# Loads moved ahead of phase barriers, and weight units split five and six groups ahead

## The reference, cut to what matters

```python
mod = jax.nn.silu(c) @ w_ada[l] + b_ada[l]
shift, scale, gate = jnp.split(mod[:, None, :].astype(F32), 3, axis=-1)
h = (rms_norm(x, g_pre[l]) * (1.0 + scale) + shift).astype(x.dtype)
if l % 2 == 0:
    y, s1, s2 = mixer_ab(h, ...)   # gated linear attention and retention, 4 + 4 heads
else:
    y, s1, s2 = mixer_c(h, ...)    # causal convolution of width 4, then gated delta rule
x = (x.astype(F32) + gate * rms_norm(y, g_post[l])).astype(x.dtype)
```

## Time and profile before

| | us |
|---|---|
| median of 3 runs | 2666.85 (2664.86 to 2667.93) |
| profiled execution, its own time | 2668.84 |
| its span, first to last instruction | 2667.1 |
| PE busy in the span | 2482.0 (93%) |
| DVE busy | 1320.2 (50%) |
| ACT busy | 926.3 (35%) |
| POOL busy | 796.3 (30%) |
| mean granted clock of TensorE, share of full | 0.965 |

### The profile page before, as it was taken

The page is one execution under the profiler, slowest core; times in us unless marked ns, Lnnn a source line. Parts: engine busy times, 40 slices in busy tenths (PEclk is TensorE's granted clock), DMA queues, the critical chain, the costliest instruction groups (busy, mean ns, idle before and its releaser), DMA issues. The chain is left out here.

```text
span 2667.1 us, 53838 instructions
## 1 busy us (share of the span) xinstructions
PE 2482.0 (93%) x21052; PEld 1495.8 (56%) x21052; DVE 1320.2 (50%) x2927; ACT 926.3 (35%) x2664; POOL 796.3 (30%) x848
## 2 busy tenths in 40 slices
PE   7999999997899986989999999985899999999998
PEld 2444444444566632434444444455788787887876
DVE  3412112111687743981643626424666566665666
ACT  3534242322111113432322322234445454554541
POOL 2531001021111103551010000005555556465564
PEclk8999999998999996989999999997999999999998
DMA  8451212033544543542121111116513222231213
GB/s 294 132 157 48 83 45 75 32 117 124 209 146 157 173 162 114 162 135 77 64 72 52 64 52 52 56 48 174 136 58 107 63 81 89 65 105 57 81 46 92
DMA packets 256585, 270.37 MB, mean 101 GB/s; under 512 B 31223, under 2 KB 189959, under 8 KB 256378
## 3 DMA queue, kind: packets, MB, share of 16 engines
q1 hardware_dynamic: 184858, 217.28, 25.1%
q10 hardware_dynamic: 71520, 50.13, 6.7%
HBM read 180.00 MB, written 87.36 MB: 100 GB/s over the span
## 5 line engine op out<-in xcount | busy, mean ns | idle before, releaser
L613 PE MATMUL inc_b<-raw_next,inc_w_hi 128*128 128x512 bf16 (+1 forms) x768 | 229.7, 381 | 0.5 <-ACT inc_taps L1977 0.5
L613 PE MATMUL inc_b<-keep,inc_w_hi 128*128 128x512 bf16 (+1 forms) x768 | 228.5, 379 | 0.0
L613 PE MATMUL inab_b<-inab_wt,keep 128*128 128x512 f16 x768 | 167.1, 379 | 4.3 <-POOL inab_wt L562 4.1
L613 PE MATMUL inab_b<-inab_wt,inab_h 128*128 128x512 f16 x768 | 166.4, 379 | 0.0
L1131 PE MATMUL mixab_y<-keep,mixab_oT_hi 128*128 128x512 f16 x512 | 152.5, 379 | 7.9 <-DVE mixab_f_y L1211 6.2
L2089 DVE SCALAR_TENSOR_TENSOR inc_acc<-inc_ub,inc_taps,inc_acc 128x512 f32<-128x512 f32 x192 | 152.1, 792 | 6.8
L2085 DVE COPY inc_ub<-inc_halo 128x3 f32<-128x3 f32 x96 | 21.5, 223 | 252.6 <-ACT inc_ub L1996 252.6
L613 PE MATMUL inc_b<-raw_next,inc_w_lo 128*128 128x512 bf16 x384 | 146.1, 381 | 0.0
L613 PE MATMUL inc_b<-keep,inc_w_lo 128*128 128x512 bf16 x384 | 145.6, 379 | 0.0
L1996 ACT ACTIVATE inc_ub<-inc_b 128x512 f32<-128x512 f32 x96 | 57.0, 594 | 252.6 <-PE inc_b L613 252.6
L613 PEld LDWEIGHTS inab_b<-inab_wt,keep 128*128 128x128 bf16 (+1 forms) x768 | 74.8, 98 | 95.6 <-issue 6.0
(11 more groups left out here) (523 smaller groups left out, 6108.5 us busy)
## 6 DMA issues: line engine op xcount, KB each, us to landing
tmp_qkv<-inc_so SPq DMA_DIRECT2D x96, 256.0 KB, 2.0
mixc_qkv<-tmp_qkv SPq DMA_DIRECT2D x15, 1536.0 KB, 7.7
inc_stage<-in_w_in_c ACTq DMA_DIRECT2D x32, 512.0 KB, 4.5
inab_stage<-in_w_in_ab ACTq DMA_DIRECT2D x24, 512.0 KB, 4.1
mixab_cw<-in_w_ada ACTq DMA_DIRECT2D x6, 2048.0 KB, 14.6
inab_wt<-in_w_ada SPq DMA_DIRECT2D x10, 1024.0 KB, 14.5
keep<-in_x_prompt SPq DMA_DIRECT2D x16, 512.0 KB, 4.2
tmp_v<-inab_vz SPq DMA_DIRECT2D x32, 256.0 KB, 3.9
```

Of the source, the lines that this page charges most:

```text
L613: last = nc.tensor.matmul(dst, lhs(a, k), rhs(b, k), start=(k == 0 and i == 0), stop=(k == KT - 1 and i == len(PASSES) - 1))
```

## The change

- `load_tables` joins names that lie side by side in HBM into one transfer (new function `runs`), and the names are reordered for it: 3 transfers become 1 and 7 become 1 in phase_in_ab, 7 names become 4 in 2 transfers in phase_mix_ab, 3 names become 2 in 1 transfer in phase_in_c. The tables ident, sel and sel_s stay resident in `tab0`.
- `raw_next` is allocated in phase_in_ab, in place of inab_h, and takes the first tile of phase_mix_ab ahead of the barrier (a third buffer); tile 2 is loaded at the start of phase_mix_ab.
- `stage_next` is allocated in phase_mix_ab, in place of the first ring tile, and takes units 0 and 1 of w_in_c and the rows of conv_c once four pieces of w_ada are multiplied. In phase_in_c it is also the room of inc_so and inc_zb.
- The waits of PE for tables at the start of both phases go; in phase_in_c one stands later.
- In groups 3 and 10 of the first block two units are split (`TWICE`), so from group 3 on the split is five groups ahead and from group 10 on six.

```diff
 def load_tables(eng, sem, dst, names, table_d):
...
+    for c0, w in runs(names):
+        eng.dma_start(dst[:, at:at + w], table_d[:, c0:c0 + w]).then_inc(sem, 16)
+        at += w
+
+
+def runs(names):
+
+    out = []
     for n in names:
         c0, w = TABLE[n]
-        eng.dma_start(dst[:, at:at + w], table_d[:, c0:c0 + w]).then_inc(sem, 16)
-        at += w
+        if out and sum(out[-1]) == c0:
+            out[-1] = (out[-1][0], out[-1][1] + w)
+        else:
+            out.append((c0, w))
+    return out
...
-    first_names = ["ident", "sel", "sel_s"]
+    first_names = ["sel", "sel_s", "ident"]
...
+    raw_next = io["raw_next"] = io["keep"].enter_context(nc.sbuf_tensor("raw_next", [P, KT, BLK], F32))
...
+    pre = [raw_flat[:, i * D:(i + 1) * D] for i in range(3)] + [raw_flat[:, 3 * D:3 * D + 8]]
+    io["first_tile"] = pre
...
         outputs(nb - 1, BLK, TPB, [])
         rot_load(nb, NS)
+        sp.wait_ge(mm, G * nb)
+        for i in range(4):
+            sp.wait_ge(vz_out[i], 16 + 16 * TPB)
+        sp.dma_start(pre[0].rearrange("p (g n) -> p g n", g=8), io["qk0"][:, :, 0:P].rearrange("g p n -> p g n")).then_inc(pre_in, 16)
+        sp.dma_start(pre[1], io["v0"][0:P, :]).then_inc(pre_in, 16)
+        sp.dma_start(pre[2], io["z0"][0:P, :]).then_inc(pre_in, 16)
+        sp.dma_start(pre[3], io["dec0"][:, 0, :]).then_inc(pre_in, 16)
         outputs(nb, NS, 1, [])
+        sp.wait_ge(pre_in, 64)
...
+def in_c_stages(room):
+
+    flat = room[:].rearrange("p k n -> p (k n)")
+    return [flat[:, i * D:(i + 1) * D].rearrange("p (k n) -> p k n", k=KT) for i in range(2)], flat[:, 2 * D:3 * D]
...
-    names = ["ident", "incl", "incl_s", "seq", "sel", "sel_s", "eye_h"]
+    names = ["incl", "incl_s", "seq", "eye_h"]
...
-        load_tile(sp, 0, 0, P)
+        sp.sem_inc(tile_in[0], 64)
         load_tables(sp, tab_in, tab, names, io["table"])
         load_tile(sp, 1, 1, P)
...
+        load_tile(sp, 2, 0, P)
...
-        turn(0, 0, 0, P, P)
...
         fin.load_sample(sp, io["x_sample"], io["gate_s"][0], 0, gate_in)
+        stages, rows_c = in_c_stages(stage_next)
+        sp.wait_ge(cond.mm, 4)
+        for unit, stage in enumerate(stages):
+            sp.dma_start(stage, io["w_in_c"].rearrange("(k p) n -> p k n", p=P)[:, :, unit * P:(unit + 1) * P]).then_inc(next_in, 16)
+        for i in range(3):
+            sp.dma_start(rows_c[32 * i:32 * i + CONV, :], io["conv_c"][:, i * D:(i + 1) * D]).then_inc(next_in, 16)
...
     def _(pe):
-        pe.wait_ge(tab_in, 16 * len(names))
         ident = tv["ident"]
...
-            tile(t, t, 0)
+            tile(t, (2, 1)[t], 0)
...
+    TWICE = (3, 10)
+    units_at = [range(AHEAD + g + sum(t < g for t in TWICE), AHEAD + g + 1 + sum(t <= g for t in TWICE)) for g in range(G)]
...
         prep.first_tiles_done(sp)
         load_tables(sp, tab_in, tab, names, io["table"])
-        for i in range(3):
-            sp.dma_start(rows[32 * i:32 * i + CONV, :], io["conv_c"][:, i * D:(i + 1) * D]).then_inc(rows_in, 16)
+        sp.sem_inc(rows_in, 48)
+        for i in range(2):
+            sp.sem_inc(weights.stage_in[i], 16)
...
-            weights.lo(pool, AHEAD + g)
+            for u in units_at[g]:
+                weights.lo(pool, u)
...
-        for unit in range(weights.slots - 1):
-            weights.load(act, unit)
-        weights.hi(act, 0)
+        weights.hi(act, 0, False)
...
                 if first:
-                    weights.hi(act, AHEAD + g)
+                    for u in units_at[g]:
+                        weights.hi(act, u)
```

More of the change, by code:

```diff
@@ L945, in _ @@
             cond.add(dve, n)
-        dve.wait_ge(tab_in, 16 * len(names))
+        dve.wait_ge(tab_in, 16 * len(runs(names)))
         for g in range(2):
@@ L1017, in _ @@
     def _(pe):
-        pe.wait_ge(first_in, 16 * len(first_names))
+        pe.wait_ge(first_in, 16 * len(runs(first_names)))
         pe.wait_ge(silu, 1)
@@ L1029, in _ @@
         cond.pair(pe, 2)
-        pe.wait_ge(tab_in, 16 * len(names))
+        pe.wait_ge(tab_in, 16 * len(runs(names)))
         pe.wait_ge(small_in, 32)
@@ L1321, in phase_mix_ab @@
     dec = [ph.sb(f"dec{i}", [P, 8]) for i in range(2)]
+    for room, a, g in zip((qk, v, z), io["first_tile"], (8, H, H)):
+        room.append(a.rearrange("p (g n) -> p g n", g=g))
+    dec.append(io["first_tile"][3])
     ktok = ph.sb("ktok", [P, PAIRS, P])
@@ L1356, in phase_mix_ab @@
     cT = ph.sb("cT", [P, KT, C9])
-    cT_in, vm_ready = s("cT_in"), s("vm_ready")
-    ring = [ph.sb(f"cw{i}", [P, KT, 512]) for i in range(3)]
+    cT_in, vm_ready, next_in = s("cT_in"), s("vm_ready"), s("next_in")
+    ring = [stage_next] + [ph.sb(f"cw{i}", [P, KT, 512]) for i in (1, 2)]
     exn = ph.sb("exn", [P, D])
@@ L1624, in _ @@
                 dve.wait_ge(gate_in, 16)
-            tile(t, t % 2, t // 2)
+            tile(t, t % 2 if t else 2, t // 2)
         with dve.Fori(2, nt // 2) as i:
@@ L1818, in phase_in_c @@
     nb, nt = seq // BLK, seq // P
-    names = ["ident", "incl", "incl_s"]
+    names = ["incl", "incl_s"]
     tab = ph.sb("tab", [P, width(names)])
-    tv = table_views(tab, names)
+    tv = {**io["first_tables"], **table_views(tab, names)}
     UNITS = [(i * P, min(P, N_C - i * P)) for i in range((N_C + P - 1) // P)]
-    weights = Weights(nc, ph, io["w_in_c"], UNITS, 2)
+    stages, rows = in_c_stages(io["stage_next"])
+    weights = Weights(nc, ph, io["w_in_c"], UNITS, 2, stages)
     W = weights.w
@@ L1827, in phase_in_c @@
     acc = [ph.sb(f"acc{i}", [P, BLK]) for i in range(2)]
-    so_room = ph.sb("so", [P, 2, BLK])
-    so = [so_room[:, i, :] for i in range(2)]
-    rows = so_room[:].rearrange("p i n -> p (i n)")
+    so = [rows[:, i * BLK:(i + 1) * BLK] for i in range(2)]
     rows_s = weights.stage[0][:].rearrange("p k n -> p (k n)")
-    zb = [ph.sb(f"zb{i}", [P, 512]) for i in range(2)]
+    zb = [io["stage_next"][:].rearrange("p k n -> p (k n)")[:, 3 * D + i * 512:3 * D + (i + 1) * 512] for i in range(2)]
     halo = ph.sb("halo", [P, NCH, CONV - 1])
```

22 lines of the change are left out of this document (13 added, 9 removed).

## The result

The changed kernel took **2643.74 us** (median of 5 runs, 2641.92 to 2650.84) against 2666.85 for the kernel before, a ratio of 0.9916 with a 95% interval of 0.9901 to 0.9931. The profiled execution has a span of 2641.0 us, 26.1 less than the 2667.1 before.

| stretch | before | after | difference |
|---|---|---|---|
| start of the program to SP's first transfer of phase_mix_ab | 644.56 | 643.96 | -0.60 |
| from there to PE's first outputs (mixab_oe from mixab_sc) | 15.01 | 6.59 | -8.42 |
| from there to the first w_ada matmul of layer 1 | 278.94 | 281.25 | +2.31 |
| from there to SP's first table transfer of phase_in_c | 104.66 | 102.68 | -1.98 |
| from there to the first group of phase_in_c | 8.68 | 4.34 | -4.34 |

The account below looks back on a forecast made before the run. TensorE was taken as the bound nearly everywhere, except the starts of phase_mix_ab and phase_in_c; -0.9 - 7.0 - 4.5 + 2.3 - 5.8 - 7.65 = -23.55 from 2666.85 gave 2643.3 us, range 2634 to 2652.

Parts of the forecast that it names:

- Start of the program: Three table transfers at the program's start become one, so the loads queued behind them go out earlier: 0.9 us saved.
- First barrier: Start of phase_mix_ab: tile 0 loaded ahead and fewer table transfers start DVE's mask earlier, tables still last: 7.0 us saved.
- The 0.5 that I gave back for the clock: Start of phase_mix_ab: PE works, then rests over 4 us before its outputs at a low clock, taking 0.5 from 7.5 us.
- The rival with 4.3 us: Start of phase_mix_ab: something else of SP's queue holds tile 0 or 1, 4.3 us saved instead of 7.0; 2646.0, chance 0.06.
- Second barrier: Start of phase_in_c: weights loaded ahead, unit 0's low part is last, the first group starts 4.5 us earlier.
- Collision: Late phase_mix_ab: the early 1 MB load delays the sixth piece of w_ada, which PE awaits: 2.3 us lost.
- the new load is served behind w_ada, at no cost: Lower bound for the early load beside the sixth w_ada piece: 0 lost instead of 2.3 us.
- Unit 27: First block of phase_in_c: PE's wait for this unit's low part falls from 10.96 to 6.5 us; with clock, 5.8 saved.
- whole turn: First block of phase_in_c: each extra unit costs the chain 5.07 us, so the 5.8 us gain vanishes; 2649.1, chance 0.17.
- no slip: First block of phase_in_c: extra units do not delay the chain, 12.9 us saved instead of 5.8; 2636.2, chance 0.14.
- Unit 31: First block of phase_in_c: PE's 6.00 us wait for this unit's low part goes, with 1.65 of clock: 7.65 saved.
- The slower rival: First block of phase_in_c: DVE waits for a further low part in 18 groups, 2.12 us each; 2677.4, chance 0.03.

Follow-up runs that it names:

- e3_tile0_behind: The changed kernel with the four transfers of tile 0 of phase_mix_ab issued behind the barrier again, ahead of the two table transfers: 2651.07 us, 0.9943 to the kernel before.

## Why the prediction was right

The forecast of 2643.3 us is 0.4 from the median, and the sum of -23.55 agrees with the -23.1 of the medians. That is closer than the terms were, since some of their errors cancel, and such closeness is partly luck: five executions of the changed kernel spread over 9 us, and the two profiled ones are 26.1 us apart.

- **Start of the program, -0.9.** Not shown. The transposes that stood at 9.78 us start at 9.27, but phase_in_ab ends anywhere within 5 us in runs of the same code, and the tables merged alone gave 0.9997 (0.9988 to 1.0007).
- **First barrier, -7.0.** Measured -8.42, past my upper bound of 8.1. The step that failed is the landing of the tables, taken as 3.9 us from a row in which their queue was full; it was 2.0, and the mask was released by POOL's memset instead. The 0.5 that I gave back for the clock was not seen. The rival with 4.3 us, in which something else of SP's queue is late next, fell with it. That the tables were the last wait before was true, by 1.7 us.
- **Second barrier, -4.5.** Measured -4.34, by the step that was named: signal, high part, low part, first group.
- **Collision, +2.3.** Measured +2.17 in the wait and confirmed by undoing it. That the new load is served behind w_ada, at no cost, is excluded. SP's issue came 0.01 us ahead of ACT's, and the two queues were then served in turns, 930 packets each from 981 to 987 us. The Trainium skill ("DMA: Bandwidth & Descriptors", Queues, rings and completion order) has the DMA engines take turns between queues; the trace agrees. That it goes to the end whole held for the wait; that the chain behind it has nothing else to lose or to gain did not. The place at which the pair met DVE's products moved as well, and that was worth 3 us the other way in the profiled pair of executions.
- **Unit 27, -5.8.** The low part was forecast 136.1 us behind the first group (1183.4 less 1047.3), and ended 136.3 behind it (1175.13 less 1038.82). PE came to it 131.5 us behind the first group instead of 129.5, because it had waited 1.8 us for DVE's part of the same chain, which the forecast did not have. The group starts 136.46 us behind the first one instead of 140.48, and the low clock behind it lasts 3.00 instead of 5.97 us, half of which counts: -4.0 - 1.5 = -5.5. An extra unit costs the chain 2.6 us, against the 2.7 forecast, and not a turn of 5.07, and the rivals "whole turn" and "no slip" both fall. The reason given for the 2.7, that the stage is in flight by then, holds only in part: ACT waited 3.07 and 1.66 us for transfers around the first extra unit.
- **Unit 31, -7.65.** The wait is gone; what is left of the block's 13.15 us is 7.65. This is a remainder and was not measured by itself.
- **The slower rival.** PE waited twice in the groups up to 23, 1.8 us together; the first block alone, put into the kernel before, is faster by 13.9.

The time lies inside the range of 2634 to 2652. What the sum had no room for are the two differences by chance between single executions, where POOL's pair falls and the +2.31 us of the tiles, about 3 us each and of opposite sign in the pair that was profiled.

## What to carry to other kernels

When a wait goes away, ask at once what else the same chain would make the waiting engine wait for: a third extra unit took the wait for unit 27 away and gave it back as a wait of 4.7 us ahead of the transposes. Follow the ring of waits link by link to see which instruction is worth shortening. Take a transfer's landing time from a row whose queue is as full as it will be in the changed kernel. And before a gain of 2 or 3 us between two profiled executions is believed, cut several runs of the same code at the same points: here three stretches of unchanged code varied by as much.

## What the runs showed of the hardware

- Two POOL instructions on 128x1 elements, 0.73 us together, took 3.7 us when each met a DVE product of two SBUF tiles (1.23 and 2.28 us), and 0.73 beside a product that reads PSUM. The Trainium skill ("SBUF — State Buffer", SBUF: two separate sides) names this case, two SBUF inputs against a GpSimd instruction that reads SBUF, with the lock held for the whole instruction; the traces agree, and one wait that keeps the two apart went with a stretch 5.6 us shorter.
- Two table transfers landed in 2.0 us from an empty queue; the same two took 4.6 and 5.0 us behind the four transfers of a tile, and seven smaller ones there 3.9 each in the median. The four transfers of a tile of 128 tokens were complete 6.9 us behind the first issue in the kernel before, and 7.4 in e3_tile0_behind.
- A 2 MB transfer from ACT's queue and 1 MB from SP's, issued within 0.01 us, were served packet by packet in turns: 930 packets of each in 6 us, 1.90 MB against 0.47. The 2 MB landed in 10.03 us instead of 7.77.
- The first phase, without any edit in it, ended between 642.2 and 647.6 us in eight profiled executions with the same code for it. Its cause stays open.
